# Rolled loops of a two-block transformer kernel written out as straight code

## What is computed

```python
# first block
xn = rms_norm(x, norm_mix_g)
proj = xn @ w_in                        # branch inputs, q, k, v and 4 x 2048 gate logits
branches = einsum('bskw,kwd->bskd', ys, w_branch)   # 4 branches of width 512
gates = sigmoid(gate_logits.reshape(b, s, 4, 2048))
merged = sum(gates * branches, axis=2)
x = x + merged @ w_out
h = rms_norm(x, norm_mlp_g) @ w_mlp_up              # 2048 -> 8192
x = x + square(relu(h)) @ w_mlp_down                # 8192 -> 2048
# second block
x = x + mix @ w_out_2                               # attentions and a convolution before it
h2 = rms_norm(x, norm2_g_2)
x = x + (silu(h2 @ w_gate_2) * (h2 @ w_up_2)) @ w_down_2   # 2048 -> 5632 -> 2048
```

## Time and profile before

| what | value |
|---|---|
| median of 3 runs | 2570.49 us (2569.7 to 2571.66) |
| span of the profiled execution | 2567.6 us |
| TensorE matmul busy | 2511.2 us, 98% |
| VectorE busy | 1391.3 us, 54% |
| ScalarE busy | 1137.1 us, 44% |
| GpSimd busy | 236.8 us, 9% |
| DMA moved | 468.31 MB, mean 182 GB/s |
| mean granted TensorE clock | 0.996 of full |

### The profile page before, as it was taken

How to read it: one execution, slowest core, us unless ns; L and a number is a source line. 1 busy time by engine, 2 the same in 40 slices (tenths; PEclk the granted TensorE clock), 3 DMA queues, 4 the chain that set the end, 5 groups by cost and what they waited for, 6 DMA issues and landing times.

```text
span 2567.6 us, 29488 instructions
## 1 busy us (share of the span) xinstructions
PE 2511.2 (98%) x11496; PEld 2076.8 (81%) x11496; DVE 1391.3 (54%) x1427; ACT 1137.1 (44%) x1469; POOL 236.8 (9%) x205
## 2 busy tenths in 40 slices
PE   7999999999999999999999998999999999999999
PEld 5788888888888888788788886778888888888887
DVE  4675465564655445444444559855654444444444
ACT  4455544444444434334334447564543343434433
POOL 0210010110110000000000107510200000000000
PEclk9999999999999999999999999999999999999999
DMA  7556566666656566465565554434565565555654
GB/s 229 173 170 182 162 186 191 196 195 196 216 196 197 195 188 191 164 197 181 174 189 181 193 181 147 131 136 143 164 197 182 195 196 182 196 191 187 196 181 147
DMA packets 239564, 468.31 MB, mean 182 GB/s; under 512 B 11680, under 2 KB 14240, under 8 KB 239054
## 3 DMA queue, kind: packets, MB, share of 16 engines
q1 hardware_dynamic: 237918, 461.25, 56.5%
q10 hardware_dynamic: 1520, 5.24, 0.5%
HBM read 464.36 MB, written 2.10 MB: 182 GB/s over the span
## 4 chain that ended last, share of the span: by engine, by line
PE 92%; DVE 5%; ACT 1%; SPq 1%; issue 1%; DMA 0%; POOL 0%; DVEq 0%; ACTq 0%; POOLq 0%
PE acc L378 29%; PE acc L380 29%; PE acc L379 29%; DVE wlo L362 2%; PE tp L399 1%; DVE yT L1932 1%; PE tp L1269 1%; PE sd L1253 1%; SPq L545 0%; PE sd L1262 0%; DMA raw<-in_w_in 0%; ACT whi L356 0%; PE tp L1457 0%; PE tp L1230 0%; DVE xres L1873 0%
## 5 line engine op out<-in xcount | busy, mean ns | idle before, releaser
L362 DVE TENSOR_TENSOR wlo<-raw,whi 128x1024 fp32r<-128x1024 f32 x872 | 1076.2, 1275 | 965.8 <-ACT whi L356 965.3
L356 ACT ACTIVATE whi<-raw 128x1024 fp32r<-128x1024 f32 x872 | 872.0, 1048 | 1083.1 <-PE acc L380 1067.1
L378 PE MATMUL acc<-whi,opA_hi 128*128 128x512 f32 x1888 | 745.0, 395 | 20.4 <-DVE wlo L362 16.2
L380 PE MATMUL acc<-whi,opA_lo 128*128 128x512 f32 x1888 | 737.2, 390 | 0.0
L379 PE MATMUL acc<-wlo,opA_hi 128*128 128x512 f32 x1888 | 736.8, 390 | 0.0
L378 PE MATMUL acc<-whi,opB_hi 128*128 128x512 f32 (+1 forms) x1600 | 625.9, 391 | 12.4 <-DVE wlo L362 12.1
L380 PE MATMUL acc<-whi,opB_lo 128*128 128x512 f32 (+1 forms) x1600 | 620.5, 388 | 0.0
L379 PE MATMUL acc<-wlo,opB_hi 128*128 128x512 f32 (+1 forms) x1600 | 620.1, 388 | 0.0
L378 PEld LDWEIGHTS acc<-whi,opA_hi 128*128 128x128 f32 x1888 | 355.8, 188 | 95.8 <-DVE wlo L362 14.7
L380 PEld LDWEIGHTS acc<-whi,opA_lo 128*128 128x128 f32 x1888 | 355.6, 188 | 75.4
L379 PEld LDWEIGHTS acc<-wlo,opA_hi 128*128 128x128 f32 x1888 | 356.1, 189 | 71.8
(11 more groups left out here) (260 smaller groups left out, 860.3 us busy)
## 6 DMA issues: line engine op xcount, KB each, us to landing
raw<-in_w_in SPq DMA_DIRECT2D x124, 1024.0 KB, 5.6
raw<-in_w_mlp_up SPq DMA_DIRECT2D x64, 1024.0 KB, 5.5
raw<-in_w_mlp_down SPq DMA_DIRECT2D x64, 1024.0 KB, 5.0
raw<-in_w_gate SPq DMA_DIRECT2D x44, 1024.0 KB, 5.2
raw<-in_w_up SPq DMA_DIRECT2D x44, 1024.0 KB, 5.2
raw<-in_w_down SPq DMA_DIRECT2D x44, 1024.0 KB, 5.0
raw<-in_w_out SPq DMA_DIRECT2D x32, 1024.0 KB, 5.1
raw<-in_w_branch SPq DMA_DIRECT2D x16, 1024.0 KB, 5.1
```

What stands on the lines that cost most here:

```text
L356: eng.activation(whi[:, j % SPL, k, 0:cols], raw[:, j, k, 0:cols], ACT.Copy).then_inc(hi_split, 1)
L362: eng.tensor_tensor(wlo[:, j % SPL, k, 0:cols], raw[:, j, k, 0:cols], whi[:, j % SPL, k, 0:cols].bitcast(F32), ALU.subtract).then_inc(lo_s ...
L378: eng.matmul(o, a_hi, whi[:, s, i, 0:cols], start=first and i == 0, stop=False)
L380: mm = eng.matmul(o, a_lo, whi[:, s, i, 0:cols], start=False, stop=last and i == UK - 1)
```

## The change

In thirteen places `with <engine>.Fori(0, n) as i:` becomes `for i in range(n):`, and nothing else changes. The counter is then a Python number: every body is emitted n times, each wait compares with a constant, each load has a constant address, and there is no branch. The order of the instructions on each engine stays as it was.

```diff
@@ SyncE
-            with sp.Fori(0, 3) as i:
+            for i in range(3):
                 for k in range(NB):
                     for j in range(UN):
                         load_unit(sp, G_LOOP + k + i * 5, j, w_in, UK * j, i * NW + (IN_GATE + k * D + NW))
...
-            with sp.Fori(0, 3) as i:
+            for i in range(3):
                 down_loads(G_DLOOP + i * 8, i)
...
-            with sp.Fori(0, 2) as i:
+            for i in range(2):
                 for c in range(CH2_LOOP):
@@ GpSimd
-            with pool.Fori(0, 3) as i:
+            for i in range(3):
                 for c in range(UN):
                     squares(R_DLOOP + UN + c, i)
@@ ScalarE
-            with act.Fori(0, 2) as i:
+            for i in range(2):
                 gate_turn(i)
             gate_turn(2, last=True)
...
-            with act.Fori(0, 3) as i:
+            for i in range(3):
                 for r in range(2 * UN):
                     g = i * 8 + (G_DLOOP + r)
...
-            with act.Fori(0, 2) as i:
+            for i in range(2):
                 for r in range(LOOP2_RUNS):
@@ TensorE
-            with pe.Fori(0, 2) as i:
+            for i in range(2):
                 gate_turn(i)
             gate_turn(2, last=True)
...
-            with pe.Fori(0, 3) as i:
+            for i in range(3):
                 for r in range(2 * UN):
                     down = r < UN
...
-            with pe.Fori(0, 2) as i:
+            for i in range(2):
                 for r in range(LOOP2_RUNS):
```

More of the change, by code:

```diff
@@ L1863, in gate_turn @@
                             branch_part(i + 1, j - 1, R_LOOP + NB + j - 1, i * (5 * UN) + (G_LOOP + NB) * UN + j, i + 1)
-            with dve.Fori(0, 2) as i:
+            for i in range(2):
                 gate_turn(i)
@@ L1899, in _ @@
                         turned_lo(dve, T_HID + (c - 1) * MT, opA_hi, opA_lo, (c - 1) * CT)
-            with dve.Fori(0, 3) as i:
+            for i in range(3):
                 for r in range(2 * UN):
```

## The result

The changed kernel takes 2555.05 us (median of 4 runs, 2554.23 to 2556.97) where the kernel before takes 2571.07 us (4 runs, 2569.7 to 2571.97). The ratio is 0.9942, 95% interval 0.993 to 0.9954. The forecast was 2555.8 us, its range 2552.5 to 2563.0. The medians differ by 16.0 us and the two profiled spans by 13.8; the 14.7 us of the forecast lie between, and the runs of one kernel scatter by 2 to 3 us.

What follows compares the result with a forecast made beforehand. TensorE's matmuls, 2511.2 of 2567.6 us, were taken as the bound, so only its idle or slowed time counts. 7.24 + 6.99 + 0.51 = 14.7 us took the median from 2570.5 to 2555.8 us, range 2552.5 to 2563.0.

Steps and rivals of the forecast that it cites:

- The bound and the releaser: TensorE bounds the kernel; its idle time at two MLP back edges is code fetched after the jump, not VectorE's `wlo`.
- Steps 1 to 3: TensorE's first and second MLP back edges and the second block's back edge: 7.24, 6.99 and 0.51 us removed.
- Step 4: The gate loop's back edge: TensorE has no idle time there, so nothing is won.
- Steps 5 and 6: Register arithmetic and waits on registers, and SyncE's loads with constant addresses: nothing won from either.
- Step 7: More code to bring in, some 13 packets more on queue 14: taken as nothing, bounds nothing to 44 us.
- Rival A: MLP back edges: idle time is the wait for VectorE's remainder, or straight code fetches too late too; 2570.0 us, chance 0.07.
- Rival C: ScalarE or VectorE: slower code fetches take the stalls' place at some 13 packets, up to 2600 us; chance 0.04.
- Rival B: MLP hand-overs: only one of the two large stalls goes, a packet border leaving 7 us; 2563 us, chance 0.07.
- The rule of the skill: Instruction memory of two 16 KiB lines without reuse would stall the gate loop too, some 22 us won; the trace disagreed.

Runs made afterwards that it cites:

- e1_pe_mlp: Only TensorE's MLP loop written out, against the kernel before, the other twelve loops rolled; 2555.82 us, ratio 0.9939.
- e4_others: The ten loops of SyncE, GpSimd, ScalarE and VectorE written out, against the kernel before, TensorE's three left rolled; 2569.96 us, ratio 0.9996.
- e3_pe_all: TensorE's three loops written out, against the kernel before, all loops of the other engines left rolled; 2556.55 us, ratio 0.9943.
- s26_rolled: The kernel before, all loops rolled, with 26 do-nothing instructions more on TensorE in its first idle time; 2554.83 us, ratio 0.9945.
- e2_all_but_pe_mlp: The changed kernel with TensorE's MLP loop rolled again, everything else written out; 2555.87 us, ratio 0.9941 against the kernel before.
- s8_rolled: The kernel before, all loops rolled, with 8 do-nothing instructions more on TensorE in its first idle time; 2554.18 us, one run.
- s56_rolled: The kernel before, all loops rolled, with 56 do-nothing instructions more on TensorE in its first idle time; 2557.12 us, one run.
- e2s84_pe_mlp: The changed kernel with TensorE's MLP loop rolled again and 84 do-nothing instructions more ahead of it on TensorE; 2567.59 us, one run.

## Why the prediction was right, point by point

- *The bound and the releaser.* Right. TensorE's own late code was the stall and not VectorE's `wlo`, which the profile names: e1_pe_mlp removed it with VectorE's loop untouched, e4_others kept it with VectorE's loop written out. The idle time ends with the second packet behind the jump, and not with the jump's fetch as such.
- *Steps 1 to 3.* 7.24, 6.99 and 0.51 us forecast; 7.24, 6.99 and 0.60 us measured. The exit of the same loop as the yardstick of a hand-over without a jump was the step that carried the number.
- *Step 4*, nothing at the gate loop: right. The stretch 450 to 460 is busy throughout in both kernels.
- *Steps 5 and 6*, registers and addresses at nothing: right as far as a ratio of 0.9996 (0.9986 to 1.0005) in e4_others can tell.
- *Step 7*, more code: the cost of nothing is right, e3_pe_all and e1_pe_mlp are not faster than the changed kernel. The counts were wrong. TensorE's packets were to grow by the gate loop's four and fell from 96 to 91. I also expected about 13 packets more on queue 14 and there are 4 (34 after 30). I carried the rate of another stretch over to the loops. The built programs would have said it: ScalarE's grows from 1502 to 1898 instructions and VectorE's from 1415 to 1507, because the register instructions fall away while the repeated bodies come in.
- *Rival A* fell with e1_pe_mlp. *Rival C* fell with the result, whose time and turn distances show no new loss; e3_pe_all, without the smaller engines' straight code, is no faster. *Rival B* did not come about in the changed kernel.
- *The range*: the forecast less 1 and less 2 us is 2552.8, not 2552.5; nothing hangs on it.
- *Where the reasoning failed:* the sentence that the MLP body, 6.7 packets' worth, "is fetched again" because it is larger than the gate loop's four, and with it that straight code was what it took. The size of this body does not decide; it stays on the core in 7 packets and not in 8. (Size may still decide for others: the second block's body has 2488 instructions or 9.7 packets and no filler was seen to keep it on the core; s26_rolled brings three packets around its jump, at 2280.85, 2286.15 and 2292.14.) And a fetch behind the jump, which I took for the stall itself, costs 0.3 to 0.7 us where enough instructions stand between head and border. The kernel before had both against it. The forecast of time held because its price was read from the trace, turn to turn, and writing the loop out removes the jump, whatever its cause. That the kernel before happened to have the loop's head at the worst place was not known; it took no part in the sum. The forecast for e2_all_but_pe_mlp, made on the same reasoning, was off by its whole 14 us.
- *The rule of the skill.* The section "Instruction fetch mechanics" of the Trainium skill's "Runtime: NRT & Kernel Launch" gives two sizes, 128 KiB or 2048 instructions for TensorE and a memory of only two lines; the prediction used the second alone. Eight blocks of 256 would fit a body that stays in 7 packets and not in 8, if one block is kept for what comes next; that is a reading which no run here tests. The two lines do not fit: s26_rolled fetched nothing for two whole iterations of 6.6 packets. The section's forced fetch after a jump is there in e2_all_but_pe_mlp as well, and costs 0.5 us and not 7.

## What to carry to other kernels

Before a rolled loop is written out for speed, look at TensorE at the jump back against the loop's exit, and count the instruction queue's packets around it. Packets close together say that the code is fetched again. If there is idle time too that the profile puts down to "issue" or to an operand that was long done, the code is late. It is cured by writing that one engine's loop out (e1_pe_mlp, 15 us), or, for a body that fits into 7 packets, by a few instructions ahead of it that move its head over a packet border (s8_rolled and s26_rolled, the same 15 us, with 16600 instructions on TensorE instead of 22960). Such a cure by filler is only as lasting as the code ahead of the loop, and the same holds for the measured cost of any change that adds instructions ahead of one.

## What the runs showed of the hardware that I had not expected

- TensorE runs on without a fetch in a rolled loop of 1686 instructions if it lies in 7 packets: 78 packets in the whole run against 96. The 7 and 8 are worked out from the built program. The runs place one edge to within eight instructions (0 and 8 of filler, 92 and 100). By the same count the MLP loop's head in s56_rolled, some 50 instructions past a border, still goes without a fetch, and that of e2_all_but_pe_mlp, some 160 past one, does not; between them nothing was tried.
- Eight instructions of filler change the kernel by 0.6% (s8_rolled), in a place 1000 us away from them.
- Where the loop is fetched again, the packet behind the head's is in use 4.8 to 5.5 us after the head is due. At 0.23 us a matmul, some 21 to 24 matmuls with their weight loads ahead of the border would cover it, an estimate. It fits the second block's loop: with nine matmuls ahead of the border (s56_rolled) 2.9 us are lost against straight code, and with thirty fewer of filler, so some 24 matmuls ahead of it (s26_rolled), 0.3 us. Heads that stood farther ahead lose 0.3 to 0.7 us (e2_all_but_pe_mlp, and the second block's loop in the kernel before and in e1_pe_mlp).
- Of 7.24 us lost at the first hand-over, 5.29 us were the wait and 2 us the matmuls behind it, started 0.43 us apart at the 1.2 GHz level. The length of the wait alone does not set this second part. In e2s84_pe_mlp the matmuls behind the first wait, 3.23 us, start 0.23 us apart throughout (1042.73, 1042.96), and behind the second, 3.27 us, they start 0.43 us apart from 1225.39 to 1228.38, at the 1.2 GHz level (granted clock 0.50 in 1225.5 to 1228.3, against 1.00 in 1042.8 to 1046); that is why its hand-overs take 26.31 and 27.97 us. In e4_others hand-overs of 29.57 and 31.08 us have waits of 5.20 and 5.31 us in the same way.
